# The embedding's projection of a three-block kernel, made in sixteen halves beside the last local unit and the layer norm behind it

## The chip, the cores and the metric

The kernel runs on one core of one Trainium2 chip. The metric is the device time of one execution in microseconds, and lower is better. The core has five engines: TensorE (PE in the rows; PEld is its weight load), VectorE (DVE), ScalarE (ACT), GpSimd (POOL) and SyncE (SP). TensorE writes into accumulators ("acc" in the rows, eight banks of 128x512 fp32), and the others work mostly in the on-chip memory.

## What is computed

Three transformer blocks follow each other on 1024 tokens of width 1024. The change touches only the second, whose end is this (cut):

```python
def _hybrid_layer(x, p_i, w_in, ..., w_out, ln1_g, ln1_b, w_ffn_in, w_ffn_out, ln2_g, ln2_b, w_ple_gate, w_ple_proj):
    ...
    h_m = _mlstm_group(...)                      # four heads of width 128
    h_a = _window_gqa(q, k, v, attn_sink)        # 8 query heads, window of 128 to each side
    mix = jnp.concatenate([h_m, h_a], axis=-1) @ w_out
    x = _layer_norm(ALPHA * x + mix, ln1_g, ln1_b)
    gate_ff, up_ff = jnp.split(x @ w_ffn_in, 2, axis=-1)
    ffn = (jax.nn.silu(gate_ff) * up_ff) @ w_ffn_out
    ple = jax.nn.sigmoid(x @ w_ple_gate) * (p_i @ w_ple_proj)
    return _layer_norm(ALPHA * x + ffn + ple, ln2_g, ln2_b)
```

`p_i` is an embedding of width 256 for every token, and `w_ple_proj` is 256x1024. The projection `p_i @ w_ple_proj` depends on nothing else in the block, so it may be made at any time before the gates are multiplied with it. Everything is fp32.

## The kernel before

**Layout.** Everything is kept as features x tokens: a tile is 128 features (partitions) by 1024 tokens, and `h`, the running sum, has `KT` = 8 tiles. An fp32 product is made of three faster ones. Each operand is split into a rounded part and the rest (`x_hi`, `x_lo`; `w_hi`, `w_lo`), and TensorE makes hi x hi, lo x hi and hi x lo. So a product of one 128x128 weight tile with one tile is 6 matmuls of 128x512, 3 for each half of the tokens.

**Weights.** They come in one stream of blocks of eight 128x128 tiles in the order in which TensorE uses them (`second_blocks`, L2187, gives the order for this block). SyncE loads a block into one of two `raw` slots, GpSimd splits it into `w_hi` and `w_lo` (two operations of 128x1024), and TensorE raises `w_used` with the first matmul of a block. GpSimd splits block b into the slot of block b-2 once b blocks are counted in `w_used`, which means once block b-1 is begun. A "feature block" is the product of one block with all eight tiles of x (one output tile). A "row block" (`row_block`, L455) takes one 128-wide operand and makes all eight output tiles, which VectorE adds to `h` one by one (L896).

**Accumulators.** A product goes into one of two slots of two banks each. `claim` waits until the slot's last content is taken. The other four banks hold, in attention, the turned probabilities (three banks) and the values' sum (one bank).

**The local units.** `window_tensor` (L1604) runs the attention in four units of two heads. In a unit TensorE makes scores for eight query tiles, VectorE adds the bias and takes the maximum (L772), ScalarE makes the exponentials (L841), VectorE scales them (L784, L788), TensorE turns them with an identity matrix (L718), ScalarE copies them back (L859), and TensorE weighs the values (L742). ScalarE copies the unit's sum (L881) and rounds it, and VectorE splits off the rest. The next row block uses that operand. In units one to three TensorE makes the next unit's queries, a feature block, inside the unit's tail. The fourth unit has no such block; 12 dummy matmuls (`keep_clock`, L500 to L502) stand behind it, ahead of its row block.

**The layer norm behind it.** (`norm_tensor` L504, `norm_scalar`, `norm_vector`.) VectorE adds each product to `h` and sums the tiles into `rstd` (L599, L616). TensorE averages that over the partitions (L496), VectorE subtracts it from the eight tiles (L634), ScalarE squares them (L529), TensorE sums the squares (L471), and ScalarE makes the reciprocal root by a logarithm and an exponential with a table load before each (L521, L523). Then the rows follow: VectorE scales (L648), ScalarE adds the offset, keeps a scaled copy and rounds (L584, L587, L481), VectorE splits off the rest (L486), and TensorE starts the feed-forward with the tiles as they come (L424). Between these steps TensorE makes 20, 9 and 38 dummy matmuls.

**The projection.** It stands behind the feed-forward: `ple_tensor` (L1654) makes 14 dummy matmuls, waits for the split operand and makes two row blocks with two operand tiles each, eight products in all; then come eight gate blocks. `ple_scalar` (L1662) loads `p_rows`, rounds it and copies each product into `ple` (L1671). `ple_vector` (L1685) makes `p_lo`.

The order on each engine is that of the code, written out by hand. There is no scheduler.

## Time and profile before

| | us |
|---|---|
| median of three runs | 3579.7 |
| lowest and highest | 3577.6, 3581.3 |
| the profiled execution | 3578.2 |
| its span | 3576.4 |
| TensorE busy | 3432.6 |
| VectorE busy | 1701.7 |
| GpSimd busy | 1202.8 |
| ScalarE busy | 777.6 |
| mean granted clock of TensorE | 0.988 of full speed |

How to read it. The page gives busy times and a chain: from the last instruction of the program it goes back, at each step, to what released it. A timeline row has the start, the length, the engine, the line, the operation with its output and inputs, and how many operations are run together in the row; in brackets stands how long the engine was idle before, and who ended the wait. Matmuls overlap, so a row's length is a little more than the distance to the next one. Dummy matmuls (L502) count as busy TensorE time.

### The profile page before, as it was taken

What the parts mean: (1) busy time and instruction counts of PE and PEld (TensorE: products, weight loads), DVE (VectorE), ACT (ScalarE), POOL (GpSimd) and SP (SyncE); (2) the same over time, 40 slices, a digit from 0 to 9 for tenths busy, and PEclk for the clock granted to TensorE, in tenths of its full rate; (3) what the DMA queues carried; (4) which work ended last, traced back from release to release, by engine and by line L of the source; (5) the groups of instructions that cost most, each with busy time, mean ns of one, the idle gap of its engine ahead of it and who ended that gap; (6) DMA issues with size and microseconds to landing.
All of it is one profiled execution on the core that took longest, in us unless ns stands there. A gap on an engine that the chain in (4) does not pass through costs nothing.

```text
span 3576.4 us, 41017 instructions
## 1 busy us (share of the span) xinstructions
PE 3432.6 (96%) x16540; PEld 2738.6 (77%) x16540; DVE 1701.7 (48%) x2042; ACT 777.6 (22%) x1154; POOL 1202.8 (34%) x534
## 2 busy tenths in 40 slices
PE   7999999989999999989999999999999999999997
PEld 5777877778888888867886668888888877766675
DVE  4423533362322222488766743223232257988835
ACT  3433100020000000142224440000000113144352
POOL 2122444424343334332331123443334332433322
PEclk9999999999999999999999999999999999999998
DMA  2111211101111111121211001111111110111111
GB/s 96 37 39 38 89 47 47 47 30 53 47 47 47 52 47 47 41 67 53 83 46 33 23 30 47 47 47 51 49 47 47 59 35 25 58 40 40 41 36 65
DMA packets 47295, 171.82 MB, mean 48 GB/s; under 512 B 5472, under 2 KB 6112, under 8 KB 47200
## 3 DMA queue, kind: packets, MB, share of 16 engines
q1 hardware_dynamic: 38016, 138.43, 11.8%
q10 hardware_dynamic: 9184, 32.03, 2.6%
q8 instruction: 72, 1.18, 0.1%
q14 instruction: 23, 0.19, 0.0%
HBM read 165.71 MB, written 4.72 MB: 48 GB/s over the span
## 4 chain that ended last, share of the span: by engine, by line
PE 85%; DVE 8%; ACT 3%; issue 3%; POOL 1%; DMA 0%; ACTq 0%; DVEq 0%; POOLq 0%
PE acc L387 70%; PE acc L405 4%; PE acc L742 2%; PE acc L718 2%; PE acc L424 1%; DVE conv_slots L1736 1%; PE acc L471 1%; DVE rstd L616 1%; PE acc L695 1%; DVE normed L648 1%; PE acc L707 1%; DVE x_lo L486 0%; DVE h L896 0%; POOL w_lo L2051 0%; DVE window_scores L772 0%
## 5 line engine op out<-in xcount | busy, mean ns | idle before, releaser
L2037 POOL TENSOR_TENSOR w_hi<-raw,zero 128x1024 fp32r<-128x1024 f32 x264 | 517.5, 1960 | 2317.4 <-PE acc L387 1657.1
L387 PE MATMUL acc<-x_hi,w_hi 128*128 128x512 f32 x2512 | 778.3, 391 | 5.7 <-POOL w_lo L2051 3.1
L387 PE MATMUL acc<-x_lo,w_hi 128*128 128x512 f32 x2512 | 774.3, 389 | 0.0
L387 PE MATMUL acc<-x_hi,w_lo 128*128 128x512 f32 x2512 | 774.1, 389 | 0.0
L2051 POOL TENSOR_TENSOR w_lo<-raw,w_hi 128x1024 fp32r<-128x1024 f32 x262 | 678.9, 2591 | 20.6
L896 DVE TENSOR_TENSOR h<-h,acc 128x1024 f32<-128x1024 f32 x312 | 380.6, 1221 | 554.5 <-PE acc L387 553.9
L387 PEld LDWEIGHTS acc<-x_hi,w_hi 128*128 128x128 f32 x2512 | 470.1, 188 | 106.6 <-POOL w_lo L2051 4.7
L387 PEld LDWEIGHTS acc<-x_lo,w_hi 128*128 128x128 f32 x2512 | 471.9, 188 | 98.5
L387 PEld LDWEIGHTS acc<-x_hi,w_lo 128*128 128x128 f32 x2512 | 471.9, 188 | 98.4
L1163 DVE TENSOR_TENSOR hid<-act_g,acc 128x1024 f32<-128x1024 f32 x44 | 53.7, 1221 | 570.8 <-PE acc L387 554.7
L481 ACT ACTIVATE hid_hi<-hid 128x1024 fp32r<-128x1024 f32 x44 | 46.7, 1062 | 909.3 <-DVE hid L1163 909.3
L1736 DVE SCALAR_TENSOR_TENSOR conv_slots<-conv_slots,par 128x1024 f32<-128x1024 f32 x120 | 227.5, 1896 | 4.2
L387 PE MATMUL acc<-hid_hi,w_hi 128*128 128x512 f32 x704 | 217.1, 390 | 0.7 <-DVE hid_lo L486 0.7
L387 PE MATMUL acc<-hid_lo,w_hi 128*128 128x512 f32 x704 | 216.8, 389 | 0.0
L387 PE MATMUL acc<-hid_hi,w_lo 128*128 128x512 f32 x704 | 216.8, 389 | 0.0
L486 DVE TENSOR_TENSOR hid_lo<-hid,hid_hi 128x1024 fp32r<-128x1024 f32 x44 | 138.1, 3139 | 49.9 <-ACT hid_hi L481 49.9
L387 PEld LDWEIGHTS acc<-hid_hi,w_hi 128*128 128x128 f32 x704 | 131.9, 188 | 28.5 <-DVE hid_lo L486 1.1
L387 PEld LDWEIGHTS acc<-hid_lo,w_hi 128*128 128x128 f32 x704 | 132.2, 188 | 27.5
L387 PEld LDWEIGHTS acc<-hid_hi,w_lo 128*128 128x128 f32 x704 | 132.2, 188 | 27.4
L1139 ACT ACTIVATE act_g<-acc 128x1024 f32<-128x1024 f32 x44 | 45.2, 1028 | 360.1 <-PE acc L387 360.1
L502 PE MATMUL acc<-ident,mean_w 128*128 128x128 f32 x812 | 96.4, 280 | 16.6 <-DMA h<-x_t 16.6
L502 PEld LDWEIGHTS acc<-ident,mean_w 128*128 128x128 f32 x812 | 95.9, 196 | 21.4 <-issue 20.6
(331 smaller groups left out, 3945.8 us busy)
## 6 DMA issues: line engine op xcount, KB each, us to landing
raw<-blocks SPq DMA_DIRECT2D x264, 512.0 KB, 3.4
h<-x_t ACTq DMA_DIRECT2D x8, 512.0 KB, 8.6
h<-x_t ACTq DMA_DIRECT2D x1, 4096.0 KB, 15.5
q_past<-q_dram ACTq DMA_DIRECT2D x8, 512.0 KB, 5.4
w_own<-r_dram ACTq DMA_DIRECT2D x8, 512.0 KB, 6.5
out_t<-out_rows ACTq DMA_DIRECT2D x8, 512.0 KB, 3.0
near_bias<-bias ACTq DMA_DIRECT2D x4, 896.0 KB, 4.6
band_bias<-bias ACTq DMA_DIRECT2D x4, 640.0 KB, 3.8
```

The costliest lines, as they stand in the source:

```text
L387: ins = pe.matmul(acc[s][:, c], w[:, slot, tile, :], part[:, c], start=(n == 0 and m == 0), stop=(n == last and m == 2))
L405: ins = pe.matmul(acc[s][:, c], w[:, slot, k, :], part[:, k, c], start=(k == 0 and m == 0), stop=(k == KT - 1 and m == 2))
L481: act.activation(hi, source, ACT.Copy).then_inc(hi_ready, 1)
L486: dve.tensor_tensor(lo, source, hi.bitcast(F32), ALU.subtract).then_inc(lo_ready, 1)
L502: pe.matmul(acc_all[:, 2 * TOK:2 * TOK + P], mean_w[:, :], ident[:, :], start=True, stop=True)
L718: return pe.transpose(turned[bank][0:w, at * P:(at + 1) * P], a.probs[:, p % 2, side, sink + c * P:sink + c * P + w], ident[:, :])
L742: ins = pe.matmul(att_out[rows_of(side), p % 4 * P:(p % 4 + 1) * P], a.v_tok[0:w, first // P + c, rows_of(side)], a.probs_t[0:w, p % 2, si ...
L896: dve.tensor_tensor(h[:, j, :], h[:, j, :], acc[s], ALU.add).then_inc(acc_free[s], 1)
L1163: dve.tensor_tensor(hid[:, :], act_g[:, :], acc[s], ALU.mult).then_inc(acc_free[s], 1)
L1736: ins = dve.scalar_tensor_tensor(out=out, in0=shifted, scalar=weight, in1=out, op0=ALU.mult, op1=ALU.add)
L2037: pool.tensor_tensor(hi, whole, nothing, ALU.add).then_inc(hi_split, 1)
L2051: pool.tensor_tensor(lo, whole, hi.bitcast(F32), ALU.subtract).then_inc(w_split, 1)
```

## The change

- The projection moves. Its eight products are made as 16 halves of 512 tokens (`ple_parts`), 6 matmuls each, into the four banks beside the slots: half 0 in the fourth unit ahead of the last turned probabilities, halves 1 and 2 behind the unit, 3 to 5 behind its row block, 6 and 7 behind the mean, 8 to 15 behind the sum of squares. There are no dummy matmuls in these places any more, nor behind the feed-forward.
- ScalarE copies halves 0 to 7, 11 and 12 to 15 into `ple`, VectorE 8 to 10.
- The operand is loaded and rounded by ScalarE when the fourth unit's queries are taken. VectorE makes `p_lo` between the fourth and the fifth add of the row block ahead of that unit. `p_hi`, `p_rows` and `p_lo` lie where the upper half of `x_lo` is written later, so VectorE waits for the sixteenth half before it writes the fifth tile of `x_lo`.
- The projection's two weight blocks move in the stream to both sides of the fourth unit's row block. `release_blocks`, a small dummy matmul, raises `w_used` by 1 ahead of the fourth unit and by 2 behind half 7, so that the slots of blocks that are done are split anew although the next block is not begun.

```diff
-        p_rows = at("p_rows", 120, [P, 2, TOK])
-        p_hi = at("p_hi", 176, [P, 2, TOK], F32R)
-        p_lo = at("p_lo", 184, [P, 2, TOK], F32R)
+        p_hi = at("p_hi", 72, [P, 2, TOK], F32R)
+        p_rows = at("p_rows", 80, [P, 2, TOK])
+        p_lo = at("p_lo", 80, [P, 2, TOK], F32R)
...
+        def release_blocks(pe, t, n):
+            s = claim(pe, t)
+            pe.matmul(acc[s][:, 0:P], mean_w[:, :], ident[:, :], start=True, stop=True).then_inc(w_used, n)
+
+        ple_banks = [acc_all[:, (4 + b) * HALF:(5 + b) * HALF] for b in (2, 0, 1, 3)]
+
+        def ple_parts(pe, slot, first, after):
+            for i in range(first, after):
+                if 4 <= i < 12:
+                    pe.wait_ge(ple_taken, i - 3)
+                elif 12 <= i < 15:
+                    pe.wait_ge(ple_moved, i - 11)
+                elif i == 15:
+                    pe.wait_ge(ple_taken, 9)
+                c = slice(i % 2 * HALF, (i % 2 + 1) * HALF)
+                for k in range(2):
+                    for m, (w, part) in enumerate(((w_hi, p_hi), (w_hi, p_lo), (w_lo, p_hi))):
+                        ins = pe.matmul(ple_banks[i % 4], w[:, slot, i // 2 % 4 * 2 + k, :], part[:, k, c],
+                                        start=(k == 0 and m == 0), stop=(k == 1 and m == 2))
+                ins.then_inc(ple_full, 1)
+
+        def ple_beside_norm(pe, t, slot):
+            def parts(stage):
+                if stage == 0:
+                    ple_parts(pe, slot, 3, 6)
+                elif stage == 1:
+                    ple_parts(pe, slot, 6, 8)
+                    release_blocks(pe, t, 2)
+                else:
+                    ple_parts(pe, take_block(pe, t), 8, 16)
+            return parts
+
+        def take_ple(act, first, after):
+            for i in range(first, after):
+                act.wait_ge(ple_full, i + 1)
+                act.activation(ple[:, i // 2, i % 2 * HALF:(i % 2 + 1) * HALF], ple_banks[i % 4], ACT.Copy)\
+                   .then_inc(ple_taken, 1)
+
+        def take_ple_beside_norm(act):
+            def parts(stage):
+                first, after = ((3, 6), (6, 8), (11, 12))[stage]
+                take_ple(act, first, after)
+            return parts
+
+        def move_ple(dve):
+            for i in range(8, 11):
+                dve.wait_ge(ple_full, i + 1)
+                dve.tensor_copy(ple[:, i // 2, i % 2 * HALF:(i % 2 + 1) * HALF], ple_banks[i % 4])\
+                   .then_inc(ple_moved, 1)
...
+                if beside is not None and k - 1 == KT // 2:
+                    dve.wait_ge(ple_full, PLE_PARTS)
...
-                att_tensor(pe, t, local, keys_2, next_block=n < HEAD_PAIRS - 1, joint=True, sink=1)
-            keep_clock(pe, 12)
+                if n < HEAD_PAIRS - 1:
+                    att_tensor(pe, t, local, keys_2, joint=True, sink=1)
+            release_blocks(pe, t, 1)
+            await_parts(pe, t, 2)
+            slot = take_block(pe, t)
+            att_tensor(pe, t, local, keys_2, next_block=False, joint=True, sink=1,
+                       beside=lambda: ple_parts(pe, slot, 0, 1))
+            ple_parts(pe, slot, 1, 3)
             await_parts(pe, t, 1)
-            row_block(pe, t, [(att2_hi[:, :], att2_lo[:, :])])
+            row_block(pe, t, [(att2_hi[:, :], att2_lo[:, :])], release=False)
+            return slot
...
+                if n == HEAD_PAIRS - 1:
+                    act.dma_start(p_rows[:, :, :], p_t.rearrange("(k p) n -> p k n", p=P)).then_inc(p_in, 16)
+                    act.wait_ge(p_in, 16)
+                    for k in range(2):
+                        split_hi(act, t, p_rows[:, k, :], p_hi[:, k, :])
+                        t.next("lo_ready")
...
+                    for j in range(KT):
+                        add_row(dve, t, j)
+                        if n == HEAD_PAIRS - 1 and j == 3:
+                            for k in range(2):
+                                split_lo(dve, t, p_rows[:, k, :], p_hi[:, k, :], p_lo[:, k, :])
...
-            keep_clock(pe, 14)
-            await_parts(pe, t, 2)
-            row_block(pe, t, [(p_hi[:, k, :], p_lo[:, k, :]) for k in range(2)])
...
-            norm_tensor(pe, t, (20, 9, 38), centre=True)
+            norm_tensor(pe, t, (0, 0, 0), centre=True, beside=ple_beside_norm(pe, t, slot))
...
-            norm_scalar(act, t, ch, "keep", centre=True, rows=True, eps="eps5", beta="ln1_b")
+            norm_scalar(act, t, ch, "keep", centre=True, rows=True, eps="eps5", beta="ln1_b",
+                        beside=take_ple_beside_norm(act))
+            take_ple(act, 12, 16)
...
-            norm_vector(dve, t, ch, "keep", "ln1_g", centre=True, rows=True)
+            norm_vector(dve, t, ch, "keep", "ln1_g", centre=True, rows=True, beside=lambda: move_ple(dve))
...
+        if n == HEAD_PAIRS:
+            yield ple_blocks[0]
         if n:
             yield from row_blocks(out_heads[:, n - 1].reshape(P, D), 0)
+    yield ple_blocks[1]
     yield from ffn_blocks(w_ffn_in, w_ffn_out)
-    yield from row_blocks(w_ple_proj, 0, 2)
```

What stands in a row on an engine, at three places. First VectorE in the row block ahead of the fourth unit, before (`h` is the running sum, `acc` an accumulator slot, `att_lo` the rest of the third unit's operand):

```order
L486 TENSOR_TENSOR att_lo<-local_att_sum,att_hi 128x1024 [waits hi_ready]
L896 TENSOR_TENSOR h<-h,acc 128x1024 [waits acc_full0]
L896 TENSOR_TENSOR h<-h,acc 128x1024 [waits acc_full1]
L896 TENSOR_TENSOR h<-h,acc 128x1024 [waits acc_full0]
L896 TENSOR_TENSOR h<-h,acc 128x1024 [waits acc_full1]
L896 TENSOR_TENSOR h<-h,acc 128x1024 [waits acc_full0]
L896 TENSOR_TENSOR h<-h,acc 128x1024 [waits acc_full1]
```

and now:

```order
L489 TENSOR_TENSOR att_lo<-local_att_sum,att_hi 128x1024 [waits hi_ready]
L967 TENSOR_TENSOR h<-h,acc 128x1024 [waits acc_full0]
L967 TENSOR_TENSOR h<-h,acc 128x1024 [waits acc_full1]
L967 TENSOR_TENSOR h<-h,acc 128x1024 [waits acc_full0]
L967 TENSOR_TENSOR h<-h,acc 128x1024 [waits acc_full1]
L489 TENSOR_TENSOR p_lo<-p_rows,p_hi 128x1024 [waits hi_ready] x2
L967 TENSOR_TENSOR h<-h,acc 128x1024 [waits acc_full0]
```

The two subtractions that make `p_lo` now stand between the fourth and the fifth add.

Second, TensorE at the end of the fourth unit, before (`local_probs` are turned into `local_probs_t` by the identity `ident`; L742 weighs the values `local_v_tok`; `mean_w` with `ident` is the dummy):

```order
L742 MATMUL acc<-local_probs_t,local_v_tok 64x128 x6
L718 MATMUL acc<-ident,local_probs 128x128 [waits turned_copied,p_ready]
L718 MATMUL acc<-ident,local_probs 128x128
L718 MATMUL acc<-ident,local_probs 128x128 [waits turned_copied,p_ready]
L718 MATMUL acc<-ident,local_probs 128x128
L742 MATMUL acc<-local_probs_t,local_v_tok 64x128 x6
L742 MATMUL acc<-local_probs_t,local_v_tok 64x128 [waits turned_copied]
L742 MATMUL acc<-local_probs_t,local_v_tok 64x128 x3
L502 MATMUL acc<-ident,mean_w 128x128 x12
L387 MATMUL acc<-att_hi,w_hi 128x512 [waits acc_free0,w_split,lo_ready]
```

and now, from the same value matmuls on:

```order
L811 MATMUL acc<-local_probs_t,local_v_tok 64x128 x6
L524 MATMUL acc<-p_hi,w_hi 128x512
L524 MATMUL acc<-p_lo,w_hi 128x512
L524 MATMUL acc<-p_hi,w_lo 128x512
L524 MATMUL acc<-p_hi,w_hi 128x512
L524 MATMUL acc<-p_lo,w_hi 128x512
L524 MATMUL acc<-p_hi,w_lo 128x512
L787 MATMUL acc<-ident,local_probs 128x128 [waits turned_copied,p_ready]
L787 MATMUL acc<-ident,local_probs 128x128
L787 MATMUL acc<-ident,local_probs 128x128 [waits turned_copied,p_ready]
L787 MATMUL acc<-ident,local_probs 128x128
L811 MATMUL acc<-local_probs_t,local_v_tok 64x128 x6
```

One half of the projection, six matmuls, stands ahead of the last tile's transposes. The 12 dummies are gone; two halves stand in their place, behind the last value matmuls.

Third, VectorE in the layer norm, from the last sum into `rstd` to the first rows, before (`par` holds the gains):

```order
L616 TENSOR_TENSOR rstd<-rstd,h 128x1024 [waits v_chain,acc_free1]
L634 TENSOR_TENSOR h<-h,acc 128x1024 [waits acc_full0]
L634 TENSOR_TENSOR h<-h,acc 128x1024 x7
L648 SCALAR_TENSOR_TENSOR normed<-h,par,rstd 128x1024 [waits acc_free1]
L648 SCALAR_TENSOR_TENSOR normed<-h,par,rstd 128x1024
L486 TENSOR_TENSOR x_lo<-normed,x_hi 128x1024 [waits hi_ready]
```

and now:

```order
L681 TENSOR_TENSOR rstd<-rstd,h 128x1024 [waits v_chain,acc_free1]
L699 TENSOR_TENSOR h<-h,acc 128x1024 [waits acc_full0]
L699 TENSOR_TENSOR h<-h,acc 128x1024 x7
L554 COPY ple<-acc 128x512 [waits ple_full] x3
L715 SCALAR_TENSOR_TENSOR normed<-h,par,rstd 128x1024 [waits acc_free1]
L715 SCALAR_TENSOR_TENSOR normed<-h,par,rstd 128x1024
L489 TENSOR_TENSOR x_lo<-normed,x_hi 128x1024 [waits hi_ready]
```

Three copies of halves stand between the subtraction of the mean and the first row.

## Rows read from the trace of the kernel before

**Rows 1.** The page: its busy times, and the engines' shares of the chain that ended last.
```profile
PE 3432.6 (96%) x16540; PEld 2738.6 (77%) x16540; DVE 1701.7 (48%) x2042; ACT 777.6 (22%) x1154; POOL 1202.8 (34%) x534
...
PE 85%; DVE 8%; ACT 3%; issue 3%; POOL 1%; DMA 0%; ACTq 0%; DVEq 0%; POOLq 0%
```

**Rows 2.** Timeline, feed-forward's end to gates: start us, us, engine, line, operation [idle before <-releaser].
```profile
2815.71 3.29 PE L502 MATMUL acc<-ident,mean_w 128*128 128x128 f32 x28
...
2817.05 2.35 DVE L486 TENSOR_TENSOR p_lo<-p_rows,p_hi 128x1024 fp32r<-128x1024 f32 x2
...
2819.46 0.72 PE L387 MATMUL acc<-p_hi,w_hi 128*128 128x512 f32 x2 [0.46 <-DVE p_lo L486]
...
2841.33 0.62 PE L387 MATMUL acc<-x_hi,w_hi 128*128 128x512 f32 x2
```

**Rows 3.** Timeline, ScalarE and its queue, the embedding's operand at its old place.
```profile
2793.81 0.40 ACTq L1664 DMA_DIRECT2D p_rows<-p_t  x1
2798.79 2.01 ACT L481 ACTIVATE p_hi<-p_rows 128x1024 fp32r<-128x1024 f32 x2 [6.26 <-DMA p_rows<-p_t]
```

**Rows 4.** Timeline, the row block ahead of the fourth local unit.
```profile
2000.33 1.03 ACT L1631 ACTIVATE local_queries<-acc 128x1024 f32<-128x1024 f32 x1 [3.96 <-PE acc L405]
...
2004.68 2.59 DVE L896 TENSOR_TENSOR h<-h,acc 128x1024 f32<-128x1024 f32 x2 [0.37 <-PE acc L387]
...
2007.66 1.22 DVE L896 TENSOR_TENSOR h<-h,acc 128x1024 f32<-128x1024 f32 x1 [0.39 <-PE acc L387]
```

**Rows 5.** Timeline, VectorE beside GpSimd: first stage, fourth unit's start, fourth row block.
```profile
100.33 1.89 POOL L2037 TENSOR_TENSOR w_hi<-raw,zero 128x1024 fp32r<-128x1024 f32 x1 [34.10 <-PE acc L405]
100.38 2.19 DVE L817 TENSOR_SCALAR band_probs<-band_probs,small 128x640 f32<-128x640 f32 x1
...
2015.55 0.35 DVE L788 TENSOR_SCALAR local_probs<-local_probs,small 128x256 f32<-128x256 f32 x1
...
2039.56 2.41 POOL L2051 TENSOR_TENSOR w_lo<-raw,w_hi 128x1024 fp32r<-128x1024 f32 x1
...
2040.09 1.22 DVE L599 TENSOR_TENSOR h<-h,acc 128x1024 f32<-128x1024 f32 x1 [0.16 <-PE acc L387]
```

**Rows 6.** The tile band_probs, first stage's scaling: duration ns min/median/max, first and last start.
```profile
L817 DVE TENSOR_SCALAR band_probs<-band_probs,small x64: 285/521/2191, 75.5 to 296.0; 128x640 f32<-128x640 f32 x32, 128x128 f32<-128x128 f32 x8, 128x256 f32<-128x256 f32 x8, 128x384 f32<-128x384 f32 x8
```

**Rows 7.** Timeline, TensorE at the end of the fourth unit.
```profile
2032.64 1.31 PE L742 MATMUL acc<-local_probs_t,local_v_tok 128*64 128x128 f32 x20
...
2033.88 2.94 PE L502 MATMUL acc<-ident,mean_w 128*128 128x128 f32 x24
...
2037.00 0.74 PE L387 MATMUL acc<-att_hi,w_hi 128*128 128x512 f32 x2 [0.17 <-DVE att_lo L486]
```

**Rows 8.** Timeline, the layer norm behind the units and the feed-forward's start.
```profile
2051.26 4.63 PE L502 MATMUL acc<-ident,mean_w 128*128 128x128 f32 x40
...
2056.77 1.98 PE L496 MATMUL acc<-rstd,mean_w 128*128 128x512 f32 x4 [0.88 <-DVE rstd L616]
...
2058.59 2.17 PE L502 MATMUL acc<-ident,mean_w 128*128 128x128 f32 x18
...
2061.25 13.97 PE L471 MATMUL acc<-square,mean_w 128*128 128x512 f32 x32 [0.49 <-ACT square L529]
...
2075.06 8.65 PE L502 MATMUL acc<-ident,mean_w 128*128 128x128 f32 x76
...
2075.26 1.11 ACT L521 ACTIVATE rstd<-acc,par 128x1024 f32<-128x1024 f32 x1 [1.02 <-PE acc L471]
...
2078.78 2.48 DVE L648 SCALAR_TENSOR_TENSOR normed<-h,par,rstd 128x1024 f32<-128x1024 f32 x2 [10.85 <-ACT rstd L523]
...
2084.69 0.71 PE L424 MATMUL acc<-x_hi,w_hi 128*128 128x512 f32 x2 [0.98 <-DVE x_lo L486]
```

**Rows 9.** Timeline, TensorE in the layer norm's rows.
```profile
2093.30 1.19 PE L424 MATMUL acc<-x_hi,w_hi 128*128 128x512 f32 x2 [2.88 <-DVE x_lo L486]
```

**Rows 10.** Windows: stretch, its us, busy us of each engine, granted clock, DMA share, GB/s.
```profile
2092.00:2096.00 4.00, 2.69 (x7) 2.15 (x7) 3.17 (x4) 3.91 (x4) 0.00 (x0) 0.50 0.37 131
```

53 lines of the change are left out of this document (31 added, 22 removed).

## The prediction

> **What bounds the kernel now.** I read the page first: TensorE is busy for 96% of the span and holds 85% of the chain that ended last, VectorE 8% [rows 1]. So time is won where TensorE has less work on the chain, or where work moves into its waits; and in the few stretches where it waits, the engine that it waits for sets the pace. The timeline around the embedding's projection comes next [rows 2]: behind the feed-forward's last block TensorE makes filler matmuls and waits for p_lo (2815.71 to 2819.46), then it makes the projection (2819.46 to 2841.33), then the first gate block begins. The timelines of the fourth local unit and of the layer norm [rows 4, 7, 8] show the opposite: VectorE and ScalarE set the pace, and TensorE fills with 12, 20, 9 and 38 dummy matmuls. The change carries work from the first kind of stretch into the second. The question is how much of it fits.
>
> **Gain, at the old place.** All of 2815.71 to 2841.33 goes: 14 fillers, the wait for the split and 16 halves of the projection, 25.62 us [rows 2]. The 16 halves alone are 21.87 us, so one half (6 matmuls) is 1.37 us. What is late next is the gate block's weights. GpSimd splits a block when the block before it is begun, which is a whole block (8 x 1.37 = 11 us of TensorE) ahead of need, and the split takes 1.89 and 2.41 us [rows 5], so they are there; the accumulator's other half is freed by the add that ran beside the fillers. I count the whole 25.62 us.
>
> **Loss 1, the operand's split, in the row block ahead of the fourth unit.** ScalarE issues the DMA when the queries are taken, at 2000.33 + 1.03 = 2001.36. In the old place it took 4.98 us from issue to the first p_hi, and 2.01 us for both p_hi [rows 3]: p_hi is ready at about 2008.4. ScalarE has nothing else to do until the unit's first exponentials, which come after the eighth add, so on its side this is hidden; if the cover were gone it would be the 7 us. VectorE does not. Its adds stand back to back with the products (2004.68 to 2007.27, then 2007.66 [rows 4]), and both p_lo are now put behind the fourth add. They need the first p_hi at 2007.4 and last 2.35 us [rows 2]: the fifth add starts at about 2009.8 in place of 2007.66. TensorE can't run ahead, since each product needs an accumulator that an add has freed. So the unit starts 2.1 us later. Bounds: 1.2 us if the adds catch up (each waits up to 0.4 us for its product [rows 4]), 3.5 us if the DMA meets a weight load.
>
> **Loss 2, a split that now falls into the unit.** The dummy that releases a block stands at the unit's start, so GpSimd splits the next weights there (about 2012.5 to 2014.4, and 2014.4 to 2016.8 by 1.89 and 2.41 us). The local units had no split there before, and each ran its scaling of the probabilities undisturbed. In the first stage's attention one such VectorE operation did meet a split: it began at 100.38, the split ran from 100.33 to 102.22, and the operation took 2.19 us [rows 5] against a median of 0.52 [rows 6]. An add with an accumulator as input was not held (2040.09, 1.22 us, beside the split of 2039.56). The first scaling of the fourth unit starts at 2015.55 [rows 5], so it would end about at 2017.1, not 2015.9: 1.25 us, and VectorE is the unit's pace, so it stays. The local units' own rows alone would say 0; the far row says 1.25, and I take it, since the kinds of operation are the same. The Trainium skill (SBUF — State Buffer, section "SBUF: two separate sides") says that VectorE and GpSimd hold a shared pair of ports as an exclusive lock for a whole instruction. By that rule the sum has the 1.25 us, and the trace agrees with its 2.19 us; it speaks against this place for the release.
>
> **Loss 3, the first half in the unit's tail.** Half 0 stands ahead of the last tile's transposes. TensorE works without a pause there until 2033.88 (20 value matmuls behind 4 transposes), then idles with fillers to 2037.00 while ScalarE and VectorE make the sum and its split [rows 7]. 1.37 us ahead of that tail moves it by 1.2 us (0.15 us of it was a wait for the last scaling). Halves 1 and 2 (2.74 us) fit into the 3.12 us that the fillers held: nothing.
>
> **Loss 4, the layer norm.** Halves 3 to 5 (4.11 us) take the place of 4.63 us of fillers, and TensorE waits for VectorE's sum until 2056.77 anyway [rows 8]: nothing. Halves 6 and 7 and the release (2.74 + 0.25 us) begin at 2058.59 and end at 2061.6, where the sum of squares began at 2061.25: 0.3 us. ScalarE takes two halves ahead of the logarithm, about 0.6 us each (a copy twice as wide is 1.03 [rows 4]), and it had 1.02 us of idle time there: nothing more. Behind the sum of squares halves 8, 9 and 10 end at 2075.36 + 3 x 1.37 = 2079.5, and VectorE must copy each before it may start the rows. No row shows VectorE copying 128x512 out of an accumulator; an add of 128x1024 is 1.22 us, so it lies between 0.5 and 1.22, and I take 0.65 (half of 1.22 and a start). The last copy ends at 2079.5 + 0.2 + 0.65 = 2080.35. The rows began at 2078.78 [rows 8]: 1.6 us later, the 0.3 included. Half 11 ends at 2080.8 and ScalarE has it by 2081.6, in time for the first row (2080.35 + 1.3). Halves 12 to 15 end at 2086.3; the first tile of x_lo is ready 1.6 us later than before, at 2086.2, so TensorE starts the feed-forward at 2086.3 against 2084.69: the same 1.6 us, and the splits that meet VectorE's rows afterwards keep their place against them. Bounds of this loss: 1.3 and 2.4 us.
>
> **Nothing else.** Behind the norm ScalarE takes four halves, about 2.4 us, ahead of its first table load for the feed-forward. VectorE's first product there needs TensorE's second block too, which ends later; were that cover gone, it would be the 2.4 us. Two weight splits beside the subtractions of the mean meet operations that read the accumulator, which were not held.
>
> **Sum.** 25.62 - 2.1 - 1.25 - 1.2 - 1.6 = 19.5 us. The profiled execution took 3578.2 us (its span 3576.4 and 1.8 around it), the three runs' median is 3579.7, 1.5 above. So 3558.7 for a profiled run and **3560** us for the median.
>
> **Rivals.**
> 1. *The unit's start gives it back.* The adds catch up and the collision hits an operation that has slack: losses 1 and 2 shrink to about 0.5 together, the sum is 22.3, time 3557. For it: VectorE waits 0.4 us for an add [rows 4]. Against: two p_lo are 2.35 us, and four adds follow.
> 2. *TensorE's clock falls in the fourth unit.* In the norm's rows TensorE stood idle for 2.88 us before 2093.30, behind other waits with short bursts [rows 9], and the granted clock of 2092 to 2096 was 0.50, the 1.2 GHz level [rows 10]. Now it idles for 2.2 us at the p_lo and again for over 2 us at the held scaling. One such stretch of 4 us doubles TensorE's work of the unit there: up to 2 us, with another collision or a late copy up to 4. Time 3562 to 3565. Against: its two new waits are shorter, and products and scores lie between them. The Trainium skill (TensorE: Matmul & The Clock Gate, Part 1) says that the slow clock is the default and activity releases it; by that rule the removed fillers matter only where no half stands in their place, and that is this spot.
> 3. *The gate block isn't ready.* If its weights or the accumulator were late at the old place, TensorE would wait for up to one split, 4.3 us: 3564. GpSimd's lead of one block speaks against it.
> 4. *Slower.* All 79 fillers around the norm are gone. Should the clock stand at 1.2 GHz from the sum of squares on and stay there in the feed-forward, each microsecond there loses half. It decides from 39 us at the low level (2 x 19.5); with 50 us the kernel takes 3585. The stretch of [rows 10] was about 4 us long, and the halves keep TensorE busy from 2075 to 2086, so I hold it unlikely.
>
> **Chances.** Forecast (3557.5 to 3562.5) 0.58; rival 1 0.13; rival 2 0.21; rival 3 0.05; rival 4 0.03. The range takes in rivals 1 and 2 and the copies' and DMA's bounds: 3554 to 3568. 0.2% is 7.2 us, about what a measurement of this kernel can tell from no change, so same is 3572.5 to 3586.9. Faster 0.95, same 0.03, slower 0.02.
>
> **What would show it.** In the changed profile: (a) between the feed-forward's last matmul and the first gate matmul no gap over 0.2 us; (b) in the row block ahead of the fourth unit, 2.3 to 2.5 us of p_lo and an idle TensorE behind it; (c) one scaling of about 1.5 us at the unit's start; (d) VectorE's first row of the norm released by its own third copy, not by ScalarE's exponential, and a distance of 1.5 us or so more from the end of the sum of squares; (e) TensorE without a gap from the sum of squares to the feed-forward; (f) a granted clock of 1.00 in the unit. The forecast is wrong if the fourth unit from row block to row block is longer by more than 5.5 us or less than 3.5, or if the norm grows by more than 2.5.

## The result and the profile after

The changed kernel takes 3556.64 us (median of 4 runs, 3555.48 to 3559.21) beside 3578.64 us for the kernel before on the same chip: a ratio of 0.9942, with an interval of 0.9930 to 0.9954, 22.0 us less. Forecast were 3560 us and a range of 3554 to 3568. The profiled execution has a span of 3553.8 us; before it was 3576.4, so the two profiles differ by 22.6 us where the sum of the prediction said 19.5.

Since the code ahead of the change is the same in both kernels but doesn't take the same time in each execution, all distances below are counted from one point, the first product of the row block ahead of the fourth local unit. The first rows are the timeline of the changed kernel around that row block and the unit's start (start, duration, engine, line, output and inputs; in brackets the idle time before it and who ended it). They answer to [rows 4, 5].

```profile
2000.88 0.39 ACTq L1711 DMA_DIRECT2D p_rows<-p_t  x1
...
2005.68 2.01 ACT L484 ACTIVATE p_hi<-p_rows 128x1024 fp32r<-128x1024 f32 x2 [3.78 <-DMA p_rows<-p_t]
...
2007.73 2.35 DVE L489 TENSOR_TENSOR p_lo<-p_rows,p_hi 128x1024 fp32r<-128x1024 f32 x2
...
2011.27 0.73 PE L389 MATMUL acc<-att_hi,w_hi 128*128 128x512 f32 x2 [1.72 <-DVE h L967]
...
2014.24 0.49 PE L509 MATMUL acc<-ident,mean_w 128*128 128x128 f32 x2
...
2014.82 1.89 POOL L2112 TENSOR_TENSOR w_hi<-raw,zero 128x1024 fp32r<-128x1024 f32 x1 [9.20 <-PE acc L509]
2015.47 1.27 DVE L1736 COPY window_scores<-small 128x4 f32<-128x4 f32 x1
...
2016.79 2.36 POOL L2126 TENSOR_TENSOR w_lo<-raw,w_hi 128x1024 fp32r<-128x1024 f32 x1
...
2018.86 0.44 DVE L859 TENSOR_SCALAR local_probs<-local_probs,small 128x256 f32<-128x256 f32 x1
...
2019.35 0.90 PE L787 MATMUL acc<-ident,local_probs 128*128 128x128 f32 x4 [0.71 <-DVE local_probs L859]
```

VectorE makes both p_lo at 2007.73, and TensorE stands for 1.72 us behind them (2011.27). At the unit's start GpSimd splits from 2014.82 and 2016.79, and beside the first split VectorE's copy of four columns takes 1.27 us. The unit's tail and the start of the output projection's row block, against [rows 7]:

```profile
2035.21 0.50 PE L524 MATMUL acc<-p_hi,w_hi 128*128 128x512 f32 x1
...
2036.70 0.60 PE L787 MATMUL acc<-ident,local_probs 128*128 128x128 f32 x4
...
2040.34 1.23 DVE L489 TENSOR_TENSOR att_lo<-local_att_sum,att_hi 128x1024 fp32r<-128x1024 f32 x1 [4.98 <-ACT att_hi L484]
...
2041.62 0.73 PE L389 MATMUL acc<-att_hi,w_hi 128*128 128x512 f32 x2
```

Half 0 (2035.21) stands ahead of the last transposes (2036.70); the row block starts at 2041.62. The norm, against [rows 8]:

```profile
2080.12 1.12 ACT L580 ACTIVATE rstd<-acc,par 128x1024 f32<-128x1024 f32 x1
...
2082.55 1.06 ACT L582 ACTIVATE rstd<-rstd 128x1024 f32<-128x1024 f32 x1
...
2084.20 0.69 DVE L554 COPY ple<-acc 128x512 f32<-128x512 f32 x1 [0.67 <-PE acc L524]
...
2084.81 2.47 DVE L715 SCALAR_TENSOR_TENSOR normed<-h,par,rstd 128x1024 f32<-128x1024 f32 x2
...
2090.81 0.63 PE L426 MATMUL acc<-x_hi,w_hi 128*128 128x512 f32 x2
...
2092.43 2.30 DVE L489 TENSOR_TENSOR x_lo<-normed,x_hi 128x1024 fp32r<-128x1024 f32 x1 [0.54 <-ACT x_hi L484]
...
2094.76 3.29 DVE L715 SCALAR_TENSOR_TENSOR normed<-h,par,rstd 128x1024 f32<-128x1024 f32 x1
```

The inverse root is ready at 2083.61 (2082.55 + 1.06), but the rows begin at 2084.81, behind VectorE's third copy of a half. TensorE runs halves from 2079.51 to the first tile of the feed-forward at 2090.81 without a gap. The next x_lo and the next row meet GpSimd's splits, as they did before: 2.30 and 3.29 us. The old place, against [rows 2]:

```profile
2821.32 0.62 PE L389 MATMUL acc<-hid_hi,w_lo 128*128 128x512 f32 x2
...
2821.78 0.62 PE L389 MATMUL acc<-x_hi,w_hi 128*128 128x512 f32 x2
```

Nothing stands between the feed-forward's last matmul and the gate. The gate block began at 2841.33 before and begins at 2821.78 now, 19.55 us sooner. So the sum of the four losses and the gain is nearly the forecast one there; the other 3.0 us of the 22.6 come later.

**Where the 3.0 us come from.** The distance stays at 19.55 us up to the first product of the third block (`glu_tensor`, behind a layer norm whose scaled rows are held back; first tile at 2980.13 before, 2960.58 after). From its first tile to the next product it is 31.41 us before and 28.53 us after, with the same instructions: 2.9 of the 3.0 us. The windows view of 11 us there in the kernel before (columns: window, its length, busy time and instructions of PE, PEld, DVE, ACT and POOL, the granted clock, the DMA's share, GB/s):

```profile
2984.00:2995.00 11.00, 8.91 (x21) 6.54 (x22) 10.86 (x9) 3.32 (x4) 2.37 (x1) 0.53 0.14 49
```

and the same 11 us of the changed kernel:

```profile
2964.00:2975.00 11.00, 8.75 (x32) 6.68 (x33) 10.86 (x8) 3.18 (x3) 2.81 (x1) 0.84 0.13 48
```

The granted clock was 0.53 before and 0.84 after: TensorE ran at the 1.2 GHz level from 2984.5 to 2994.7, 10.2 us, and after the change for 3.5 us only (from 2964.5). No step of the prediction looks at that place.

### The profile page after: what moved, and what is told of

Same layout as the page of the kernel before. It is cut to its first block, busy times and chain, and to the rows that moved or that the text cites. A ratio compares the mean times of both kernels' runs of the same rounds, so it can differ in the third digit from the quotient of the medians.

```text
span 3553.8 us, 40665 instructions
## 1 busy us (share of the span) xinstructions
PE 3408.1 (96%) x16358; PEld 2712.8 (76%) x16358; DVE 1704.9 (48%) x2045; ACT 776.5 (22%) x1159; POOL 1202.3 (34%) x534
## 4 chain that ended last, share of the span: by engine, by line
PE 85%; DVE 8%; ACT 3%; issue 3%; POOL 1%; DMA 0%; ACTq 0%; DVEq 0%; POOLq 0%
PE acc L389 70%; PE acc L407 4%; PE acc L811 2%; PE acc L787 2%; PE acc L426 1%; DVE conv_slots L1811 1%; PE acc L474 1%; DVE rstd L681 1%; PE acc L764 1%; DVE normed L715 1%; PE acc L776 1%; DVE h L967 0%; PE acc L524 0%; DVE x_lo L489 0%; POOL w_lo L2126 0%
## 5 line engine op out<-in xcount | busy, mean ns | idle before, releaser
L389 PEld LDWEIGHTS acc<-hid_hi,w_hi 128*128 128x128 f32 x704 | 131.9, 188 | 28.5 <-DVE hid_lo L489 1.1
L505 PE MATMUL acc<-ident,mean_w 128*128 128x128 f32 x626 | 75.0, 281 | 16.5 <-DMA h<-x_t 16.5
L505 PEld LDWEIGHTS acc<-ident,mean_w 128*128 128x128 f32 x626 | 74.8, 198 | 20.0 <-issue 19.4
```

Source lines behind the costliest of these rows:

```text
L389: ins = pe.matmul(acc[s][:, c], w[:, slot, tile, :], part[:, c], start=(n == 0 and m == 0), stop=(n == last and m == 2))
L505: pe.matmul(acc_all[:, 2 * TOK:2 * TOK + P], mean_w[:, :], ident[:, :], start=True, stop=True)
```

## The experiments

Two tables first, since the experiments are read from them. Distances in us from the first product of the fourth row block, each from the timeline of that kernel's profile. "First score" and "first transposes" are TensorE's first matmuls of that kind in the fourth unit. The feed-forward makes its first two feature blocks tile by tile, as the norm's rows come; "next feature block" is the first matmul behind these two. The last column is where TensorE was at 1.2 GHz in this stretch, and for how long, to half a microsecond.

| kernel | first score | first transposes | output row block | first row of the norm | feed-forward's third tile | its next feature block | TensorE at 1.2 GHz |
|---|---|---|---|---|---|---|---|
| before | 11.80 | 15.83 | 36.87 | 78.65 | 93.17 | 115.13 | 2090.0, 7 us |
| before_again | 11.77 | 15.80 | 36.83 | 78.57 | 93.10 | 115.06 | 2096.0, 3.5 us |
| after | 13.99 | 18.68 | 40.95 | 84.14 | 98.66 | 120.62 | none |
| after_again | 14.01 | 18.70 | 41.65 | 84.84 | 99.37 | 121.32 | 2020.5, 3.5 us; 2102.5, 3.5 us |
| half0_out | 13.98 | 18.67 | 41.93 | 85.11 | 99.64 | 121.59 | 2018.0, 7 us; 2100.0, 3.5 us |
| sink_copy_first | 13.99 | 18.68 | 40.95 | 84.13 | 98.65 | 120.63 | none |
| third_copy_late | 14.00 | 18.69 | 41.72 | 83.72 | 99.34 | 121.31 | 2021.0, 3.5 us; 2103.0, 3.5 us |
| release_in_tail | 13.68 | 17.59 | 40.09 | 83.27 | 97.78 | 120.54 | 2092.0, 10 us |
| fourth_on_vector | 14.00 | 18.69 | 40.96 | 82.95 | 98.08 | 120.66 | 2097.0, 7 us |
| lo_in_tail | 12.17 | 16.87 | 38.06 | 81.12 | 95.65 | 117.62 | none |
| lo_in_tail_filled | 12.18 | 16.86 | 38.05 | 81.14 | 95.66 | 117.61 | 2099.5, 3.5 us |
| both_in_tail | 11.86 | 15.81 | 40.22 | 83.27 | 97.78 | 119.75 | 2039.0, 3.5 us; 2097.0, 7 us |
| second_block_out | 13.99 | 18.68 | 40.95 | 82.96 | 97.47 | 119.43 | 2081.5, 17 us |

Kernels that don't differ in a stretch agree there within 0.04 us as long as the clock stands. Where it fell in the fourth unit, they differ by 0.7 to 2.2 us. In the feed-forward's first tiles a fall often costs nothing: from the third tile to the next feature block it is 21.95 to 21.97 us in after_again, half0_out and third_copy_late, which have one there, and 21.96 us in after, which has none. The point itself, from which the distances are counted, lay anywhere from 1998.3 to 2003.6 us in these profiles, though the code ahead of it is the same in all of them.

The medians (the first four kernels of the table below shared a chip, the next four another, the last four a third):

| kernel | median us | before beside it | ratio, interval |
|---|---|---|---|
| after_again | 3557.02 | 3577.70 | 0.9940 (0.9923 to 0.9957) |
| half0_out | 3553.68 | 3577.70 | 0.9930 (0.9913 to 0.9946) |
| sink_copy_first | 3556.64 | 3577.70 | 0.9942 (0.9925 to 0.9958) |
| third_copy_late | 3558.18 | 3577.70 | 0.9941 (0.9924 to 0.9958) |
| filled_before | 3576.17 | 3576.66 | 0.9999 (0.9989 to 1.0009) |
| release_in_tail | 3553.08 | 3576.66 | 0.9936 (0.9919 to 0.9952) |
| fourth_on_vector | 3554.37 | 3576.66 | 0.9940 (0.9923 to 0.9957) |
| lo_in_tail | 3553.57 | 3576.66 | 0.9935 (0.9918 to 0.9951) |
| before_again | 3576.61 | 3576.06 | 1.0001 (0.9991 to 1.0011) |
| both_in_tail | 3555.37 | 3576.06 | 0.9938 (0.9921 to 0.9954) |
| lo_in_tail_filled | 3553.49 | 3576.06 | 0.9935 (0.9919 to 0.9952) |
| second_block_out | 3550.52 | 3576.06 | 0.9928 (0.9911 to 0.9944) |

The intervals are some 12 us wide, so no median tells 1 us from another. The verdicts below rest on the distances.

### Are the 3.0 us the change's? Both kernels once more

> The changed kernel as it is, once more, as the base of the other three and as a second profile of the stretch where the trace of before and the trace of after differ by 3.0 us that no term of the prediction holds. There (the first tiles of the product behind the last held norm) before ran at 1.2 GHz for some 10 us and after for 3.6 us. Theory A (the length of the low stretch is a matter of the moment and differs from one execution to the next): this profile has a low stretch of another length than 3.6 us there, or the same within chance, and times of one kernel scatter by 2 to 4 us. Theory B (the change itself fixes it, since it moves the program in time against the chip's clock management): 3.6 us again, and a span of 3553 to 3555 us. Time 3555 to 3559 by both.

> The kernel before, once more, for a second profile of the product behind the last held norm, where the first profile has TensorE at half its clock for 10.2 us (2984.5 to 2995). Theory A (such a stretch comes at another length, or not at all, from one execution to the next, as the two profiles of the changed kernel differ there: 3.4 us and none): a length other than 10.2 us, and the 31.4 us from that product's first tile to the next product falls to 28.4 us. Theory B (the kernel before always falls there for long, and the change cures it): 10.2 us and 31.4 us again. Time 3577 to 3579 by both.

From the first tile of that product to the next product it took 28.56 us in after_again, with a clock of 1.00, and 29.94 us in before_again, with 0.69. The windows view of before_again:

```profile
2986.00:2997.00 11.00, 8.54 (x27) 6.41 (x28) 10.86 (x9) 3.17 (x3) 2.52 (x1) 0.69 0.15 49
```

and of after_again:

```profile
2966.00:2977.00 11.00, 7.30 (x31) 5.76 (x32) 10.86 (x8) 3.18 (x3) 2.99 (x1) 1.00 0.13 48
```

Theory A holds: four executions, four lengths of the low stretch (10.2 and 7 us in before, 3.5 and none after), though the second profile of before didn't fall to the 28.4 us that were expected. In the nine other profiles of changed kernels (one with fillers there) the same distance was 28.52 to 28.56 six times and 30.14 to 30.19 three times. So up to 2.9 us of the 22.6 are chance between two executions, and a part may remain: the two of before are 31.4 and 29.9, the mean of the eleven others is 29.0. Two profiles of before don't settle how large that part is.

Fillers in the waits of that product, in the kernel before:

```
-            feature_pair(pe, t, before)
+            feature_pair(pe, t, before, (18, 12))
...
+                    if k < len(fillers):
+                        keep_clock(pe, fillers[k])
```

> The kernel before, with 18 filler products behind the first tile and 12 behind the second of the product after the last held norm, in the two places where TensorE waits 2.45 and 1.89 us for VectorE. In the profile of before TensorE ran at half its clock from 2984.5 to 2994.7 there, 10.2 us, of which some 6 us in tiles that wait for nothing; in after the low stretch was 3.4 us and over when those tiles began. Theory (the 3.0 us that no term of the prediction holds are this clock alone): no low stretch there, the tiles from the third on follow each other in 0.45 us each from the start, and the span from the first tile to the first tile of the next product falls from 31.4 to 28.4 us. Rival (the fall comes whether or not the waits are filled, or the 3.0 us has another cause, as GpSimd's splits): 31.4 stays. The median against before lower by 1 to 3 us by the theory, since not each execution need have the long low stretch.

The low stretch was gone and the distance 29.40 us, not 28.4: the 18 fillers took 4.18 us where the wait was 2.45, so the third tile started 9.46 us behind the first and not 8.60, 0.9 us too late. Without that it is 28.5 us, as in the changed kernel. The clock is the cause of what was lost there (31.41 to 29.40, with 0.9 us of the fillers' own). But against the second profile of before the gain is 0.5 us, and the medians differ by 0.5 us, within their interval.

### Loss 1: the low parts in the row block

```
-                        if n == HEAD_PAIRS - 1 and j == 3:
-                            for k in range(2):
-                                split_lo(dve, t, p_rows[:, k, :], p_hi[:, k, :], p_lo[:, k, :])
...
                 joint_vector(dve, t, ch, local, keys_2, ..., 1)
+                if n == HEAD_PAIRS - 1:
+                    for k in range(2):
+                        split_lo(dve, t, p_rows[:, k, :], p_hi[:, k, :], p_lo[:, k, :])
                 split_lo(dve, t, local.total[:, :], att2_hi[:, :], att2_lo[:, :])
```

The edit needs half 0 out of the tail, as in half0_out below; TensorE waits for the two low parts behind the unit.

> The changed kernel with half 0 out of the tail (as in the run before, where the stretch from the second last weighing to the row block fell from 7.22 to 5.98 us) and VectorE's two splits of the operand's low parts moved from the fourth row block to the tail, where VectorE waits 3.7 us. Theory (the two splits of 1.17 us each hold the row block's adds, 1.77 us of it reach the end): the first score comes 1.7 to 1.8 sooner against the row block's start, at 12.2 us instead of 14.0; in the tail the two halves start 0.3 to 0.6 later, and the row block is later by 0 to 0.3. Rival (the row block of 14.0 us has another cause, as ScalarE's two splits of the high parts or the release): 14.0 stays. Whether TensorE's clock falls in the unit, as it did for 3.4 us in the second profile of the changed kernel and for 6.8 us in that of half 0, is open; the wait of 1.72 us that TensorE had in the row block would be gone.

The timeline of its tail:

```profile
2034.81 2.35 DVE L489 TENSOR_TENSOR p_lo<-p_rows,p_hi 128x1024 fp32r<-128x1024 f32 x2
...
2037.22 0.50 PE L524 MATMUL acc<-p_hi,w_hi 128*128 128x512 f32 x1 [0.35 <-DVE p_lo L489]
...
2038.64 1.23 DVE L489 TENSOR_TENSOR att_lo<-local_att_sum,att_hi 128x1024 fp32r<-128x1024 f32 x1 [1.47 <-ACT att_hi L484]
...
2040.08 0.62 PE L389 MATMUL acc<-att_hi,w_hi 128*128 128x512 f32 x2
```

The first score comes at 12.17 us instead of 13.99, 1.82 sooner, and in the tail the two low parts (2034.81, 2.35 us) end before VectorE is wanted for the unit's result (2038.64, behind an idle time of 1.47 us). TensorE's first half waits 0.35 us for them. The theory holds, and so does its size: 0.37 us are left to the kernel before, and the release's own matmul is 0.31 of them (13.99 to 13.68, below). Of all variants this one, with and without fillers, gains most that the rows show: 3.00 us at the feed-forward's next feature block (117.62 against 120.62), 1.82 here and 1.24 from half 0, less what the tail waits.

### Loss 2: GpSimd's splits at the unit's start

```
                 last = n == HEAD_PAIRS - 1
+                if last:
+                    sink_columns()
                 if n:
                     pass_acc(t)
```

> The changed kernel with the copy of two 128x4 columns, which took 1.27 us beside GpSimd's first split and 0.16 us in before, put ahead of the row block's adds in the fourth unit. Theory (that copy was held by GpSimd's split; an operation from the accumulator is not held, as the adds of 1.22 us beside other splits show): the first score of VectorE begins at once behind the last add, 1.0 to 1.2 us sooner against the end of the row block, and so does the first transpose. Rival (the first operation of VectorE that writes the memory beside the split is held, whatever it is): the first score takes 1.6 us instead of 0.49 and nothing is gained, within 0.2.

The timeline of the unit's start:

```profile
2014.26 0.48 DVE L843 CUSTOM_DVE_ANT_0 window_scores<-acc,local_bias,small 128x256 f32<-128x256 f32 x1
...
2015.49 2.36 POOL L2133 TENSOR_TENSOR w_lo<-raw,w_hi 128x1024 fp32r<-128x1024 f32 x1
...
2016.55 1.45 DVE L859 TENSOR_SCALAR local_probs<-local_probs,small 128x256 f32<-128x256 f32 x1
...
2018.06 0.90 PE L787 MATMUL acc<-ident,local_probs 128*128 128x128 f32 x4 [1.93 <-DVE local_probs L859]
```

The score did start at once (2014.26, 0.48 us, beside the first split, which ran to 2015.41), so this operation, which reads the accumulator, isn't held. But the first transposes stood at 18.68 us as in the changed kernel: now the first scaling took 1.45 us, until the second split ended at 2017.85. The theory that the copy was the cost fell, the rival was right on the result and wrong on its operation. What these two runs show is a matter of place: with two splits of 4.3 us starting at the unit's start, the first scaling doesn't end before they do, and when the copy was held instead, it had pushed the scaling to the same end. Not every operation from memory to memory is held: VectorE's reciprocal of one column, just ahead of this scaling (2016.35) and beside the same split, took 0.16 us as it does without a split. The expectation that follows says it more widely. So the release itself was moved:

```
-            release_blocks(pe, t, 1)
             await_parts(pe, t, 2)
...
-                       beside=lambda: ple_parts(pe, slot, 0, 1))
+                       beside=lambda: (release_blocks(pe, t, 1), ple_parts(pe, slot, 0, 1)))
```

> The changed kernel with the release of the output projection's last block put into the tail, ahead of half 0, where VectorE has written its last probabilities. GpSimd's two splits (4.3 us) then run where VectorE waits 5 us for the tail, and no longer at the unit's start. Copying the sink's columns sooner had only passed the hold on to the first scaling (1.45 us instead of 0.35), so theory: what costs is that VectorE's first operation from memory to memory behind GpSimd's two splits can't end before they do; with the splits elsewhere the first transposes come 1.1 us sooner against the row block, at 17.6 us instead of 18.7, and the tail costs nothing more. Rival (the splits hold the tail's own operations, the part of the unit's result or ScalarE's copies, or the block is late for the row block): 0, or the row block 0.5 to 1.5 later in the tail.

The timeline at the unit's start:

```profile
2015.67 0.35 DVE L859 TENSOR_SCALAR local_probs<-local_probs,small 128x256 f32<-128x256 f32 x1
...
2016.08 0.90 PE L787 MATMUL acc<-ident,local_probs 128*128 128x128 f32 x4 [0.72 <-DVE local_probs L859]
```

and in the tail:

```profile
2032.51 1.89 POOL L2111 TENSOR_TENSOR w_hi<-raw,zero 128x1024 fp32r<-128x1024 f32 x1 [29.07 <-PE acc L509]
...
2034.48 2.38 POOL L2125 TENSOR_TENSOR w_lo<-raw,w_hi 128x1024 fp32r<-128x1024 f32 x1
...
2037.30 1.23 DVE L489 TENSOR_TENSOR att_lo<-local_att_sum,att_hi 128x1024 fp32r<-128x1024 f32 x1 [5.20 <-ACT att_hi L484]
```

The scaling takes 0.35 us again and the first transposes come at 17.59 us, 1.09 sooner. In the tail GpSimd's splits (2032.51 to 2036.86) end before VectorE makes att_lo (2037.30, 1.23 us), so nothing is held there; the tail is 0.23 us longer with the release's matmul in it, and 0.86 us are left at the output row block. At the next feature block only 0.08 us of that is left (120.54): from the third tile on it takes 22.76 us here and 21.96 us in after. TensorE was at 1.2 GHz for 10 us from 2092.0, which may be the cause. Loss 2 is shown at the first transposes: 1.09 us.

Both moves together, as an edit of lo_in_tail:

```
-            release_blocks(pe, t, 1)
             slot = take_block(pe, t)
-            att_tensor(pe, t, local, keys_2, next_block=False, joint=True, sink=1)
+            att_tensor(pe, t, local, keys_2, next_block=False, joint=True, sink=1,
+                       beside=lambda: release_blocks(pe, t, 1))
```

> The kernel with the low parts split in the tail and, besides, the release of the output projection's last block in the tail as well, ahead of the last transposes. Apart, the two gained 1.8 and 0.9 us. Theory (VectorE's and GpSimd's operations from memory to memory don't run side by side): the unit's start gains 1.1 us again (first transposes at 15.8 us from the row block's start, 16.9 without), but in the tail 2.35 us of low parts, 1.23 us of the result's and 4.3 us of GpSimd's splits stand in turn, where 3.7 us were free, so the tail grows by 1.5 to 3 us and the row block of the output projection starts at 38.5 to 39.9 us, later than the 38.1 us without the second move. Rival (they run side by side, the held operations seen so far have another cause): 37.0 us.

The timeline of the tail:

```profile
2035.30 4.05 DVE L489 TENSOR_TENSOR p_lo<-p_rows,p_hi 128x1024 fp32r<-128x1024 f32 x2
...
2035.79 2.47 POOL L2113 TENSOR_TENSOR w_hi<-raw,zero 128x1024 fp32r<-128x1024 f32 x1 [27.29 <-PE acc L509]
...
2038.34 3.22 POOL L2127 TENSOR_TENSOR w_lo<-raw,w_hi 128x1024 fp32r<-128x1024 f32 x1
2039.27 3.38 DVE L489 TENSOR_TENSOR att_lo<-local_att_sum,att_hi 128x1024 fp32r<-128x1024 f32 x1
2039.40 0.80 PE L524 MATMUL acc<-p_hi,w_hi 128*128 128x512 f32 x1 [1.98 <-DVE p_lo L489]
...
2043.79 0.62 PE L389 MATMUL acc<-att_hi,w_hi 128*128 128x512 f32 x2
```

The two low parts take 4.05 us instead of 2.35, att_lo 3.38 instead of 1.23, and GpSimd is held as well: 2.47 and 3.22 us instead of 1.89 and 2.38. The output row block starts at 40.22 us, 2.16 later than without the second move, though the unit's start had gained 1.06. The expected bound of 39.9 is passed by 0.3, and that is the clock, not the hold: TensorE was at 1.2 GHz from 2039.0 for 3.5 us, so the two halves took 4.39 us (2039.40 to 2043.79) where they took 2.86 in lo_in_tail (2037.22 to 2040.08), and they ended last. att_lo was there at 2042.65. With the clock up the row block would have started right behind it, at about 39.1 us (an estimate from these rows), so some 1.1 of the 2.16 us are the hold's. Two moves into the same wait, each good alone, are still worse than one. The Trainium skill (SBUF — State Buffer, section "SBUF: two separate sides") says that whoever of VectorE and GpSimd starts first keeps the shared ports for its whole instruction and the other fully blocks; of VectorE's operations it counts those with two inputs from the memory, as these are, and those in a mode that reads through two ports. By that rule the durations add up, and these rows agree: the operations of both engines last from 2035.30 to 2042.65, 7.35 us, and unheld they are 2.35 + 1.23 + 1.89 + 2.38 = 7.85 us, so only some 0.5 us of them ran side by side.

### Loss 3: half 0 in the tail

```
             att_tensor(pe, t, local, keys_2, next_block=False, joint=True, sink=1,
-                       beside=lambda: ple_parts(pe, slot, 0, 1))
-            ple_parts(pe, slot, 1, 3)
+            ple_parts(pe, slot, 0, 2)
...
-                    ple_parts(pe, slot, 3, 6)
+                    ple_parts(pe, slot, 2, 6)
```

> The changed kernel with the first half taken out of the unit's tail: halves 0 and 1 behind the unit, halves 2 to 5 ahead of the mean instead of 3 to 5. Theory (the tail is a chain, half 0 stands in it): the last transposes follow the second last weighing without the 1.27 us, the projection's row block begins 1.2 us sooner against the first transposes of the unit; the mean waits 1.27 us after the third half, so a fourth half of 1.37 us costs 0.1 to 0.2 there. Sum sooner by 1.0 to 1.1 us at the first tile of the feed-forward. Rival (the tail is bound by the chain over ScalarE and VectorE anyway, half 0 was free and the 1.24 has another cause): 0, or later by 0.1.

The timeline of its tail:

```profile
2035.65 0.88 PE L811 MATMUL acc<-local_probs_t,local_v_tok 128*64 128x128 f32 x12
...
2040.36 1.22 DVE L489 TENSOR_TENSOR att_lo<-local_att_sum,att_hi 128x1024 fp32r<-128x1024 f32 x1 [3.74 <-ACT att_hi L484]
...
2041.63 0.73 PE L389 MATMUL acc<-att_hi,w_hi 128*128 128x512 f32 x2
```

From the second last weighing to the row block it is 5.98 us (2035.65 to 2041.63) where it was 7.22 (2034.40 to 2041.62): 1.24 us sooner, as the theory has it. The fourth half ahead of the mean cost nothing, since from the row block to the mean it is 19.74 us in place of 19.75. Yet the table shows the row block at 41.93 us, 0.98 later than after. That is the clock: up to here the two kernels have the same code, and TensorE stood at 1.2 GHz from 2018.0 to 2025.0 in this execution, in the unit's first third.

The windows view of that stretch:

```profile
2017.00:2026.00 9.00, 8.29 (x38) 4.22 (x38) 6.69 (x27) 6.05 (x19) 1.16 (x1) 0.62 0.18 58
```

The second last weighing came 2.2 us late by it. after_again lost 0.70 us in the same place to 3.5 us of low clock.

### Loss 4: the norm

```
+                if beside is not None and k == 0:
+                    beside(10, 11)
```

> The changed kernel with the third of VectorE's copies of halves put behind the first of the norm's rows. Theory (the rows waited for TensorE's third half, since the inverse root was there 1.2 us before): the first row begins within 0.1 us of the inverse root, 1.1 to 1.2 sooner against the logarithm, and the third tile of the feed-forward is sooner by the same; TensorE, which runs the halves without a gap up to the first tile, delays that first tile only, which has 2.4 us of slack to the second. Rival (the halves on TensorE are the bound, since they end just as the first tile starts): 0 to 0.3 at the third tile.

The timeline of the norm's first row:

```profile
2085.06 1.06 ACT L582 ACTIVATE rstd<-rstd 128x1024 f32<-128x1024 f32 x1
...
2086.15 1.28 DVE L715 SCALAR_TENSOR_TENSOR normed<-h,par,rstd 128x1024 f32<-128x1024 f32 x1
...
2088.57 1.14 ACT L649 ACTIVATE normed<-normed,par 128x1024 f32<-128x1024 f32 x1
```

The first row follows the inverse root at once (2086.15), 1.19 us sooner against the row block (42.00 us behind it in place of 43.19). But ScalarE starts on it only at 2088.57, behind its own copy of half 11, and the third tile is only 0.1 us sooner against the row block (57.62 against 57.72 in after_again). So the theory holds for the row and fails at the tile; the rival's size came, but the holder was ScalarE's copy, which neither named. So that copy was given to VectorE too:

```
-                elif 12 <= i < 15:
+                elif 12 <= i:
                     pe.wait_ge(ple_moved, i - 11)
-                elif i == 15:
-                    pe.wait_ge(ple_taken, 9)
...
-                    beside(10, 11)
+                    beside(10, 12)
```

(The next expectation tells one old distance wrongly: from the exponential's start to the first row it was 2.26 us, and it is 1.09 with the third copy moved.)

> The changed kernel with the third of VectorE's copies of halves behind the first of the norm's rows and ScalarE's copy of half 11 given to VectorE too. With the third copy alone moved, the first row came 1.12 us sooner (1.34 to 1.36 us behind the exponential's start before, at 1.09 now), but ScalarE, which stood at its copy of half 11 until TensorE had it, began on the row only then, and nothing was gained at the third tile. Theory (two holders stood side by side): the third tile comes 1.1 to 1.2 us sooner against the logarithm, at 18.1 us instead of 19.2. Rival (TensorE's halves without a gap are the next holder): 0 to 0.5.

The timeline from the first row to the third tile:

```profile
2083.03 1.28 DVE L713 SCALAR_TENSOR_TENSOR normed<-h,par,rstd 128x1024 f32<-128x1024 f32 x1
...
2090.75 2.88 POOL L2112 TENSOR_TENSOR w_hi<-raw,zero 128x1024 fp32r<-128x1024 f32 x1 [16.21 <-PE acc L426]
...
2091.91 2.80 DVE L713 SCALAR_TENSOR_TENSOR normed<-h,par,rstd 128x1024 f32<-128x1024 f32 x1
...
2094.63 3.38 DVE L489 TENSOR_TENSOR x_lo<-normed,x_hi 128x1024 fp32r<-128x1024 f32 x1
...
2098.16 1.19 PE L426 MATMUL acc<-x_hi,w_hi 128*128 128x512 f32 x2 [4.58 <-DVE x_lo L489]
```

The first row is 1.19 us sooner, the third tile only 0.58, and the next feature block not at all (120.66), with TensorE at 1.2 GHz for 7 us from 2097.0. The only two kernels that lose time between the third tile and the next feature block, this one (0.6 us) and release_in_tail (0.8), are those whose low stretch reaches furthest behind the third tile, 5.8 and 4.7 us, against 4 at most elsewhere; so the clock is the likely cause, but no run separates it. GpSimd's splits still start with the first tile (2090.75), which TensorE's halves hold at its old place, so they meet other operations of VectorE: the rows' product takes 2.80 us and x_lo 3.38 us, 3.67 us of hold together where it was 3.08 (2.30 and 3.29 against 1.23 and 1.28). The theory of two holders is right but not whole: behind them stand TensorE's halves, which set where GpSimd's splits fall.

The last test takes all of it away at once:

```
-                    ple_parts(pe, take_block(pe, t), 8, 16)
+                    take_block(pe, t)
```

> The changed kernel without halves 8 to 15: it leaves out the second block's products and their copies, and adds the first four tiles of the projection twice, so the output is not the reference's. Theory (of what the norm loses against before, 1.41 us, the three copies ahead of the rows are 1.17 us, and the rest stands ahead of the sum of squares): the first row follows the inverse root within 0.1 us, 1.17 sooner, and the first and the third tile of the feed-forward come 1.2 sooner, at 88.9 and 97.5 us from the fourth row block's start instead of 90.1 and 98.7 us. GpSimd's splits move with the first tile here and keep their place against the rows, unlike with the fourth copy on VectorE, where the rows came 1.2 us sooner, the splits did not, and the held operations took 0.6 us of it back. Rival (the norm has a third holder): the first tile under 0.5 us sooner.

The timeline of its norm:

```profile
2081.28 2.48 DVE L715 SCALAR_TENSOR_TENSOR normed<-h,par,rstd 128x1024 f32<-128x1024 f32 x2 [11.10 <-ACT rstd L582]
...
2087.18 1.19 PE L426 MATMUL acc<-x_hi,w_hi 128*128 128x512 f32 x2 [9.46 <-DVE x_lo L489]
```

The first row is 1.18 us sooner (82.96 against 84.14), the first tile 1.28, the third tile 1.19, the next feature block 1.19, as expected. The rest of the norm's loss lies ahead of the logarithm. TensorE stood at 1.2 GHz for 17 us here, in which it waits for VectorE, and nothing of that reaches the next feature block. The median is 25.5 us below that of the kernel before beside it, where the changed kernel's was 22.0 and 20.7: 3.5 to 4.8 us more, of which the rows show 1.2 in the norm. The rest I can't assign; it lies within the intervals.

### A version with fillers

> The kernel with the low parts split in the tail and half 0 out of it, and with fillers in the two waits of the product behind the last held norm: 9 and 6, since a filler took 0.232 us there and 18 and 12 were 1.0 us too long. Theory (the clock in that stretch is the only thing that the fillers change): no low stretch there, 28.4 us from the product's first tile to the next product, and the same everywhere else as without fillers; where an execution without them has no long low stretch there, they gain nothing. So the median is that of the kernel without them, 3553.6, less 0 to 1 us. Rival (the fillers push the fall of the clock to a later place where it costs): 3553.6 or more, with a new low stretch in the next 100 us.

No low stretch at the product, 28.54 us there, against 28.56 without fillers. The median is 3553.49 against 3553.57, and no new low stretch followed in the next 100 us. As expected, nothing is gained where the long low stretch is absent. So **lo_in_tail** is the version to keep. Its rows are 3.0 us better than the changed kernel's, and its ratio to before is 0.9935 against 0.9940 and 0.9942, which the intervals don't separate; half0_out, which has only one of its two edits, has 0.9930. The choice rests on the rows.

## Why the prediction was right

**The gain, 25.62 us**, came in full: no gap at 2821.78 (point a). With the four losses as measured the sum is 25.62 - 5.50 = 20.1 us; at the gate's start 19.55 are seen, since the changed execution had begun the stretch 0.54 us later. The losses were forecast as 6.15 us together.

**Loss 1**, forecast 2.1, was 1.77 (the first score is 2.19 us late, but 0.3 to 0.4 of that is the release's matmul): the order of events was right, the two p_lo lasted 2.35 us, and the wait behind them was 1.72 us (point b). The step that was a little off is the fifth add: the DMA was issued beside the copy of the queries, not behind it, so p_hi began at 2005.68, 1.2 us sooner than forecast (2006.34, and 0.54 for the later start), and the fifth add came 1.8 us late, not 2.1. The 3.5 us for a DMA that meets a weight load come from no row; in the eleven profiles of changed kernels p_hi began 5.0 to 5.5 us behind the fourth row block's start, where the forecast has 6.2, so the DMA was never late.

**Loss 2**, forecast 1.25, was 1.08. The mechanism was right, but the operation was not, so point c didn't come: the held one was the copy of the sink's columns, 1.27 us for 128x4 elements, and the scaling took 0.44 us, since it started (2018.86) only 0.3 us before the second split ended. The prediction looked for the first scaling and left out the copy ahead of it. That the size is near all the same is no luck: with the copy out of the way the scaling was held, as forecast, and the transposes came at the same 18.68 us.

**Loss 3**, forecast 1.2, was 1.24. Halves 1 and 2 fit, as told.

**Loss 4**, forecast 1.6, was 1.41: 0.31 at the start of the sum of squares, forecast 0.3, of which 0.24 is left at the logarithm, and 1.17 at the copies. The one cost without a row, VectorE's copy of a half, was taken as 0.65 and is 0.69. Point d holds: the rows follow the third copy. Point e holds too.

**Nothing else** held anything up in the norm and behind it: ScalarE's last four halves ended before its table load for the feed-forward, whose first product still waited for TensorE's second block.

**The fourth unit** from row block to row block grew by 4.08 us, inside the 3.5 to 5.5 that were named, the norm by 1.41.

**Rival 2**, the clock falling in the fourth unit, was given 0.21. It does happen: not in the first profile of the changed kernel (point f), but in the second, and in two of the six variants that keep the row block's wait (half0_out, third_copy_late). Its price was mostly too high: it costs 0.7 us with 3.5 us of low clock and 2.2 with 7, where the prediction said up to 2 for a stretch of 4, and 2 to 5 in its times. In the three changed kernels without the wait for p_lo, and in the three profiles of the kernel before, the clock stood in the unit's first two thirds. That fits the prediction's cause, but with falls in three of the eight profiles that have the wait, six without one are few. **Rivals 1, 3 and 4** didn't come: the adds didn't catch up, the gate was ready, and TensorE's low stretches ended within 6 us behind the feed-forward's third tile. (Rival 4's 79 fillers take in the 12 of the unit's tail; 67 stood around the norm.)

**What the prediction had no term for** is the scatter between executions. The median of the first comparison was 22.0 us lower, the second 20.7 (3577.70 to 3557.02), the sum of rows 20.1. The forecast of 3560 was 3.4 us too high. 1.1 of it is the kernel before, which measured 3578.64 beside the change and not the 3579.7 of the three runs known then; 0.6 is the terms; the remaining 1.7 or so no term holds, and it is of the size of the chance between executions seen at the third block's first product. So the terms were right by their mechanism, and where in the range the median fell is in part luck.

## What to carry to other kernels

Work that is moved into an engine's waits costs where it stands in front of something, not by its length: 16 halves of 21.9 us cost 1.24 + 1.41 us in their new places, and the small things that came with them, a 2.35 us split and one release, cost 1.77 + 1.08. When two engines hold each other, moving the held operation passed the hold to the next one here; moving what holds gained 1.09 us. Add up the lengths on both engines before two such moves go into one wait. And compare two profiles only from a common point just ahead of the change, with the granted clock beside it: between executions of the same code that point moved by 5 us, and a single product took from 28.5 to 31.4.

## What was not expected of the hardware

A copy of 128x4 elements from memory to memory takes 1.27 us beside a split of GpSimd and 0.16 without, so how long an operation is held has nothing to do with its size. VectorE's operations that read the accumulator (the score, 0.48 us; the adds, 1.22) ran beside the same splits unheld, and so did a reciprocal of one column that stays in the memory (0.16). GpSimd's splits are held too (3.22 us in place of 2.38).

TensorE's clock fell to 1.2 GHz in the same stretch of the same program for 10.2, 7, 3.5 us or not at all. What the engine did ahead of it was the same each time (but for the two kernels with fillers there): a tile of 1.6 us between waits of 0.74 and 2.45 us. Where it waited for VectorE anyway, as in second_block_out for 17 us, this cost nothing; at the third block's first product it cost nothing with 3.5 us early in the product, and 1.4 to 2.9 us otherwise. The Trainium skill (TensorE: Matmul & The Clock Gate, Part 1) says that the chip's watch on the engine's activity runs free of the program, so that the same kernel can meet it differently in each run. By that rule two profiles of one kernel can differ in such places, and the trace agrees: 31.41 and 29.94 us for before.
